# Reordered work at the seams of a two-block transformer kernel on one core

## The reference, cut to what matters

```python
for layer in range(2):
    mem_k, mem_v = split(mem @ w_mem_kv[layer])            # 256 memory tokens, 4 heads
    seq_out = hgrn2_mix(...) if layer == 0 else stick_breaking_attention(...)
    mem_out = memory_attention(qm, mem_k, mem_v)
    x = post_norm(x, concat(seq_out, mem_out) @ w_o[layer], ln_mix_g, ln_mix_b)
    x = post_norm(x, hier_moe(x, ...), ln_ffn_g, ln_ffn_b)  # 4 groups of 4 experts, 1 group and 2 experts per token
# second block
x = layer_norm_2(ALPHA_2 * x + fox_mixer(x, ...), ln_mix_g_2, ln_mix_b_2)
x = layer_norm_2(ALPHA_2 * x + conv_ffn(x, ...), ln_ffn_g_2, ln_ffn_b_2)
gate = sigmoid(x @ ple_w_gate + ple_b_gate)                 # 1024 x 1024
x = x + gate * (p @ ple_w_proj)                             # p: 256 tokens x 256, the small input
```

## Time and profile before

| what | value |
|---|---|
| median of 3 runs (lowest to highest) | 989.9 us (989.45 to 990.78) |
| profiled execution: its own time, its span | 992.38 us, 990.7 us |
| busy: PE, DVE, ACT, POOL | 97%, 73%, 57%, 4% of the span |
| read from HBM | 203.87 MB, 207 GB/s over the span |
| granted TensorE clock, mean | 0.996 of full speed |

### The profile page before, as it was taken

One profiled execution on the slowest core, in us unless ns is written; L12 is line 12 of the kernel. 1 busy time (PEld: TensorE's weight loads), 2 busy tenths in 40 slices (PEclk: granted clock), 3 DMA queues, 4 the chain that ended last, 5 costly groups with the idle time before them and its releaser, 6 DMA issues.

```text
span 990.7 us, 14556 instructions
## 1 busy us (share of the span) xinstructions
PE 959.4 (97%) x5530; PEld 818.1 (83%) x5530; DVE 727.5 (73%) x905; ACT 561.3 (57%) x629; POOL 37.8 (4%) x79
## 2 busy tenths in 40 slices
PE   8999989999999999999999999899999999999997
PEld 7978988888888779878888788679887788888886
DVE  4888885988898774645988888756565977777566
ACT  3845652577777644563677667624553756656441
POOL 8000010100000000001000000000000000000010
PEclk9999998999999999999999999999999999999999
DMA  9833336299989945431599899745452566555711
GB/s 321 278 111 128 128 100 199 79 323 356 306 302 359 357 155 186 160 96 43 170 339 342 274 352 359 256 128 185 157 191 85 183 201 205 175 175 203 250 52 42
DMA packets 151985, 205.82 MB, mean 208 GB/s; under 512 B 6896, under 2 KB 123376, under 8 KB 151920
## 3 DMA queue, kind: packets, MB, share of 16 engines
q1 hardware_dynamic: 150912, 204.24, 61.4%
q10 hardware_dynamic: 1008, 0.71, 0.2%
HBM read 203.87 MB, written 1.05 MB: 207 GB/s over the span
## 4 chain that ended last, share of the span: by engine, by line
PE 79%; DVE 10%; issue 4%; ACT 4%; DMA 2%; SPq 1%; POOL 0%; POOLq 0%; DVEq 0%; ACTq 0%
PE psum L638 77%; DVE w_lo L1961 3%; ACT w_hi L1493 1%; ACT arena L1493 1%; DMA raw<-in_a_w_in 1%; DMA raw<-in_attn_w_in 1%; DVE stats L2225 1%; SPq L281 1%; DVE x_res L2245 1%; PE psum L1117 1%; DVE x_res L2238 1%; DVE xt L1978 0%; ACT mt_hi L1493 0%; PE psum L1368 0%; DVE mt_lo L1978 0%
## 5 line engine op out<-in xcount | busy, mean ns | idle before, releaser
L1961 DVE TENSOR_TENSOR w_lo<-raw,w_hi 128x2048 fp32r<-128x2048 f32 x184 | 418.1, 2287 | 71.6 <-ACT w_hi L1493 69.8
L1493 ACT ACTIVATE w_hi<-raw 128x2048 fp32r<-128x2048 f32 (+1 forms) x186 | 353.9, 1905 | 105.0 <-PE psum L638 43.7
L638 PE MATMUL psum<-xt,w_hi 128*128 128x256 f32 (+1 forms) x1056 | 253.6, 321 | 3.8 <-DVEq L2709 1.7
L638 PE MATMUL psum<-xt,w_lo 128*128 128x256 f32 x704 | 197.1, 280 | 0.0
L638 PEld LDWEIGHTS psum<-xt,w_hi 128*128 128x128 f32 x1056 | 177.1, 190 | 20.3 <-issue 2.7
L638 PE MATMUL psum<-w_hi,mt_hi 128*128 128x512 f32 (+1 forms) x448 | 174.1, 389 | 0.2 <-issue 0.2
L638 PE MATMUL psum<-w_hi,mt_lo 128*128 128x512 f32 (+1 forms) x448 | 171.3, 382 | 0.0
L638 PE MATMUL psum<-w_lo,mt_hi 128*128 128x512 f32 (+1 forms) x448 | 171.0, 382 | 0.0
L638 PEld LDWEIGHTS psum<-xt,w_lo 128*128 128x128 f32 x704 | 133.6, 190 | 0.0
L638 PE MATMUL psum<-w_hi,xt 128*128 128x512 f32 (+1 forms) x368 | 115.2, 385 | 8.0 <-ACT mem_v L1493 3.7
L638 PEld LDWEIGHTS psum<-w_hi,mt_lo 128*128 128x128 f32 x448 | 84.2, 188 | 16.7
(11 more groups left out here) (252 smaller groups left out, 1024.1 us busy)
## 6 DMA issues: line engine op xcount, KB each, us to landing
raw<-in_w_gate SPq DMA_DIRECT2D x64, 512.0 KB, 4.9
raw<-in_w_up SPq DMA_DIRECT2D x64, 512.0 KB, 6.1
raw<-in_w_down SPq DMA_DIRECT2D x64, 512.0 KB, 6.0
raw<-in_ffn_w_up SPq DMA_DIRECT2D x44, 512.0 KB, 4.6
raw<-in_a_w_in SPq DMA_DIRECT2D x26, 512.0 KB, 6.9
raw<-in_attn_w_in SPq DMA_DIRECT2D x24, 512.0 KB, 5.9
raw<-in_ffn_w_down SPq DMA_DIRECT2D x22, 512.0 KB, 4.0
raw<-in_w_o SPq DMA_DIRECT2D x16, 512.0 KB, 4.6
```

What stands on the lines that cost most here:

```text
L638: return pe.matmul(o, l, r, start=start, stop=stop, skip_group_check=skip)
L1493: return act.activation(o, i, f, **kw)
L1961: return dve.tensor_tensor(w_half(h, w_lo), w_half(h, raw), w_half(h, w_hi).bitcast(F32), ALU.subtract).then_inc(lo_split, 1)
```

## The change

What it does, in the order of the diff below:

1. SP no longer loads ln_ffn_g and ln_ffn_b after the experts; ACT issues both loads right after it has rounded block 1 of x.
2. Slots count from 1, and a token's slot number in groups not its own is 0; one comparison over 128 x 512 builds perm, and load_max is read straight from PSUM by the reduction. PE's fill in layer 1 ahead of the gather is 7 products, not 12.
3. In the first projection the free banks are awaited one by one, and ACT copies MV1 before it rounds set 5 and any further weights.
4. The last scatter goes half by half over both blocks, and moe_done is counted for each pair of block and half; norm measures each half as it comes.
5. The small input p is transposed into bank 7 after C_Q0 and split into ht_hi and ht_lo in the attention; it leaves finish_projection and norm.
6. From u = 7 on, the projection's block 1 comes one turn earlier, and ACT and DVE round and rest the next two halves at u = 8. norm 4 rests no weight between its steps, and splits block 0 after it has shifted block 1. The fill behind the products of p waits for pp_out and is 5 products, not 6.
7. In the recurrence the logs of step 4 and the scaling of step 3 come ahead of a weight rest.
8. At the gate, one weight rest stands ahead of the scaling of block 1 and one between scaling and shift; the transposes of block 1 come inside tile 1; the fill ahead of tile 0 is 1 product, not 4; the last tile's bias is put into its bank by a product of ones, and ACT takes the sigmoid straight from PSUM.

```diff
@@ sync
-                gains(a["ln_ffn_g"][layer], a["ln_ffn_b"][layer], 2 * layer + 1)
@@ gpsimd
-            own.did(pool.iota(slot_no[:], pattern=[[1, P]], base=0, channel_multiplier=0,
+            own.did(pool.iota(slot_no[:], pattern=[[1, P]], base=1, channel_multiplier=0,
@@ tensor
+            def turn_p():
+                pe.wait_ge(p_in, 16)
+                for c in range(2):
+                    for b in range(TB):
+                        last = pe.transpose(psum[:, 7, T * c + P * b:T * c + P * b + P],
+                                            p_in_t[:, b, P * c:P * c + P], ident[:])
+                last.then_inc(tr_done, 1)
@@ project
-                for b in range(TB):
-                    free(f"O0{b}")
+                split_ready(s)
                 for half, j in ((0, 0), (0, 1)):
-                    split_ready(s + half)
                     for b in range(TB):
+                        if j == 0:
+                            free(f"O0{b}")
@@ finish_projection
-                    if layer == 2 and j == 0:
-                        pe.wait_ge(p_in, 16)
-                        turn(SETS["p"], p_in_t, 0, n=2)
@@ experts, layer 1
-                    keep_busy(12, 0)
+                    keep_busy(7, 0)
@@ scatter
-                        for b in range(TB):
-                            for n in range(2):
-                                if b == 0:
-                                    pe.wait_ge(s["y_hi"], of_group(i, q, n + 1, 2))
-                                    pe.wait_ge(s["y_lo"], of_group(i, q, n + 1, 2))
+                        for n in range(2):
+                            pe.wait_ge(s["y_hi"], of_group(i, q, n + 1, 2))
+                            pe.wait_ge(s["y_lo"], of_group(i, q, n + 1, 2))
+                            for b in range(TB):
...
-                            last.then_inc(sem("moe_done"), 1)
+                                last.then_inc(sem("moe_done"), 1)
@@ attention of the second block
             fm_half("C_Q0", xt_hi, xt_lo)
+            turn_p()
...
-                project_chunks(2, {6: (0, 1, 2), 7: (3, 4), 8: (5,), 9: (6,)}[u], 0)
-                if u >= 8:
+                if u in (7, 8):
                     pe.wait_ge(sem("fox_taken"), 6)
-                    project_chunks(2, O_ROWS[2][0], 1, (u - 8,))
+                    project_chunks(2, O_ROWS[2][0], 1, (u - 7,))
+                project_chunks(2, {6: (0, 1, 2), 7: (3,), 8: (4,), 9: (5, 6)}[u], 0)
...
-                last = row_block(AT["PP"], b, mt_hi[:, 0:2, :], mt_lo[:, 0:2, :], 4, True, True)
+                last = row_block(AT["PP"], b, ht_hi[:, 0, :, :], ht_lo[:, 0, :, :], 4, True, True)
...
-            keep_busy(6, 0)
+            pe.wait_ge(sem("pp_out"), 1)
+            keep_busy(5, 4)
@@ gate
+            def turn_second(k):
+                if k == 5:
+                    turn_block(SETS["L5"], 5, 1)
...
+            pe.wait_ge(sem("pl_bias_in"), 16)
             keep_busy(3, 4)
             turn_block(SETS["L5"], 5, 0)
-            keep_busy(4, 4)
+            mm(psum[:, GATE_BANK[-1], 0:LAST_WIDTH], ones[0:1, :], pl_bias[0:1, D - LAST_WIDTH:D], True, False, skip=True)
+            keep_busy(1, 4)
             gate_tile(0)
-            turn_block(SETS["L5"], 5, 1)
-            for n in range(1, len(GATE_TILES)):
+            gate_tile(1, turn_second)
+            for n in range(2, len(GATE_TILES)):
                 gate_tile(n)
@@ scalar
                 round_x(1)
+                for i, v in enumerate((a["ln_ffn_g"], a["ln_ffn_b"])):
+                    act.dma_start(gain[:, i, :], v[layer].rearrange("(o d) -> o d", o=1).to_broadcast([P, D]))\
+                        .then_inc(gain_in, 16)
                 round_to(base + 3)
...
+            act.wait_ge(half_used, AT["MV1"] + 1)
+            fn(mem_v[:, 1, :, :].rearrange("p m c -> p (m c)"), psum[:, 3, :], ACT.Copy).then_inc(drained_a, 1)
             split_set(5)
-            copy_unit("MV1", mem_v[:, 1, :, :].rearrange("p m c -> p (m c)"), 3)
...
+            act.wait_ge(tr_done, SETS["p"] + 1)
+            fn(ht_hi[:, 0, :, :].rearrange("p k t -> p (k t)"), psum[:, 7, :], ACT.Copy).then_inc(tr_hi, 1)
...
-            round_to(AT["UP"] + 1)
-            split_set(SETS["p"], n=2)
+                elif u == 8:
+                    round_to(AT["O2"] + 6)
...
+                    act.wait_ge(sem("gate_done"), n + 1)
+                    fn(s, psum[:, GATE_BANK[n], 0:width], ACT.Sigmoid).then_inc(sem("pl_gate"), 1)
@@ vector
-                    if 3 <= st + 1 < N_STEPS:
+                    if 3 <= st + 1 < N_STEPS and st != 3:
                         a_logs(st + 1)
-                    if st >= 3:
+                    if st >= 4:
                         a_scale(st)
...
+                if n == 0:
+                    a_logs(4)
+                    a_scale(3)
                 if h < A_HALVES[-1]:
                     split_to(h + AHEAD)
@@ norm
-                    if b and n != 5:
+                    if b and whole:
                         split_block(then, 0)
+                    if b:
                         split_to(between)
                     scale(b)
+                    if b:
+                        split_to(scaled)
                     shift(b)
+                if n == 4:
+                    split_block(then, 0)
...
-                return lambda b: dve.wait_ge(sem("moe_done"), 2 * layer + b + 1)
+                return lambda b, c: dve.wait_ge(sem("moe_done"), 4 * layer + 2 * c + b + 1)
@@ place, place_slots
-                own.link(dve.tensor_copy(r_pos.rearrange("p n g -> p (n g)"), psum[:, 6, 0:12]))
-                own.link(dve.tensor_reduce(r_mx, r_pos[:, 2, :], AX, ALU.max))
-                own.link(dve.tensor_copy(load_max[:], r_mx))
-                dve.nop().then_inc(sem("placed"), 1)
-                place(layer, None)
+                dve.tensor_reduce(load_max[:], psum[:, 6, 8:12], AX, ALU.max).then_inc(sem("placed"), 1)
+                own.link(dve.scalar_tensor_tensor(r_at.rearrange("p b g -> p (b g)"), psum[:, 6, 0:8], 1.0,
+                                                  rt[:, 64:72], ALU.add, ALU.mult))
+                place(layer, 0)
...
+                if u == 8:
+                    split_to(AT["O2"] + 5)
-            norm(4, ALPHA_2, projected(2), then=SETS["L4"], upto=AT["UP"] + 1)
+            norm(4, ALPHA_2, projected(2), then=SETS["L4"])
...
-            norm(5, ALPHA_2, downed, then=SETS["L5"], upto=HALVES)
+            norm(5, ALPHA_2, downed, then=SETS["L5"], between=AT["PG"] + 3, scaled=HALVES)
```

More of the change, by code:

```diff
@@ L1175, in experts @@
                             group(i, q, True)
-                    for b in range(TB):
-                        for c in range(2):
-                            last = mm(psum[:, 2 * b + c, :], zeros_r[:], zeros_row, False, True, skip=True)
-                        last.then_inc(sem("moe_done"), 1)
+                    for c in range(2):
+                        for b in range(TB):
+                            mm(psum[:, 2 * b + c, :], zeros_r[:], zeros_row, False, True, skip=True)\
+                                .then_inc(sem("moe_done"), 1)
                 with pe.Else():
@@ L1459, in _, with gate_tile @@
                     down_block(j, b)
-            def gate_tile(n):
+            def gate_tile(n, after=nothing):
                 b, at, width = GATE_TILES[n]
@@ L2211, in _, with norm @@
             split_to(AT["O0"] + 2)
-            def norm(n, alpha, ready, then, whole=False, between=0, upto=0):
+            def norm(n, alpha, ready, then, whole=False, between=0, upto=0, scaled=0):
                 first = 3 + 2 * n
@@ L2248, in norm @@
                 for b in range(TB):
-                    ready(b)
                     if whole:
-                        measure(b, 0)
-                        measure(b, 1)
+                        for c in range(2):
+                            ready(b, c)
+                            measure(b, c)
                     else:
+                        ready(b)
                         add(b, 0)
@@ L2278, in ready @@
                     h = AT[f"O{layer}"]
-                    split_to(h + ((6, 6), (5, 5), (5, 5))[layer][b])
-                    if b and layer == 2:
-                        split_set(SETS["p"], n=2)
+                    split_to(h + ((6, 6), (5, 5), (6, 6))[layer][b])
                     if b == 0:
@@ L2303, in place @@
             def place(layer, pair):
-                for b in range(TB):
-                    for q in range(2):
-                        g = slice(q, q + 1) if pair is None else bass.ds(pair * 2 + q, 1)
-                        last = dve.tensor_scalar(perm[:, b, P * q:P * q + P], slot_no[:], r_pos[:, b, g],
-                                                 r_og[:, b, g], ALU.is_equal, ALU.mult)
-                last.then_inc(sem(f"perm_ready{layer}"), 1)
+                at = r_at[:, :, 2 * pair:2 * pair + 2].rearrange("p b (q o) -> p b q o", o=1)
```

(6 more changed lines are left out.)

35 lines of the change are left out of this document (20 added, 15 removed).

## The result

The changed kernel takes 977.73 us (median of 4 runs, 976.75 to 979.18) against 989.81 us on the same chip; the ratio is 0.9869, 95% interval 0.9855 to 0.9883. The forecast was 977.1 us. The profiled execution has a span of 976.8 us (before 990.7).

The account below looks back on a forecast made before the run. TensorE, busy 97% of the span, was taken as the bound; terms 6.55 + 0.75 + 1.3 + 1.1 + 0.35 - 0.35 + 1.4 + 1.7 = 12.8 us off 989.9 gave 977.1 us, 8-in-10 range 973.5 to 982.3 us.

Parts of the forecast that it names:

- Part 1: First projection: copying memory values first saves 3.66 us of stall and 2.9 us of slow clock, 6.55 us.
- Part 2: First layer's recurrence: step 3 scaled ahead of a weight rest, 0.75 us saved.
- Part 3a: Expert ends: first statistic runs while PE adds the second half, 0.65 us in each layer, 1.3 us.
- Part 3b: Expert ends: scale and shift rows loaded earlier, so weights arrive sooner; 1.1 us over both layers.
- rival D: Slower: each issue on ScalarE's queue holds it until the rows have landed; 994.9 us, chance 0.03.
- Parts 4 to 7: Slots 0.35 us, small input in the attention -0.35 us, last projection 1.4 us, gate tiles 1.7 us.
- A: Clock falls once more, before the feed-forward or still in the first projection, costing 2.9 us: 980.0 us, chance 0.11.
- B: Only the large stall at the first projection goes, the small terms give nothing: 983.3 us, chance 0.08.
- C: Experts take the upstream gain back as weights come at fixed times, 7.65 us lost: 984.8 us, chance 0.05.

Follow-up runs that it names:

- mem_v_back: Changed kernel with ScalarE's old order at the first projection (set 5, a weight half, then the copy); 978.69 us, ratio 0.9886.
- copy_back: Changed kernel with ScalarE's old order and both free banks awaited ahead of the first projection's first product; 984.62 us, ratio 0.9930.
- copy_back_filled: Changed kernel with ScalarE's old copy order, both banks awaited, and 16 products of zeros ahead of that wait; 983.57 us, ratio 0.9924.
- gains_back: Changed kernel with the scale and shift rows back on SP's queue at the end of each expert layer; 980.50 us, ratio 0.9887.
- mem_v_only: Kernel before with only the memory values copied first on ScalarE and the free banks awaited one by one; 986.23 us, ratio 0.9956.
- copy_and_gains_only: Kernel before with memory values first, banks one by one, and scale and shift rows early on ScalarE's queue; 984.56 us, ratio 0.9933.
- stall_filled: Changed kernel with ScalarE's old copy order plus 16 products of zeros by TensorE ahead of the first projection; 981.21 us, ratio 0.9913.
- fill_twelve: Changed kernel with 12 products of zeros instead of 5 ahead of the feed-forward loop; 978.15 us, ratio 0.9854.
- ends_back: Changed kernel with the small input, the last projection and the gates as before; 981.50 us, ratio 0.9899.

## Why the prediction was right

**Part 1.** Stall and clock were right in size (3.95 and 2.82 against 3.66 and 2.9 us). The start came 0.3 us sooner, as the copy was over while the transposes ran. The reason given was half the story: "Afterwards the copy stands ahead of both" names ScalarE's order, while waiting for the banks one by one hides the late copy but for 0.68 us (mem_v_back). With both undone the stall is back (copy_back); whether ScalarE's order alone would do was not run. That the clock's price belongs to the stall is shown by copy_back_filled; that it is 2.9 us is true of one execution, and 1.58, 2.40 and 2.82 us are what three showed. One reading was thinner than I took it for: the window of the earlier trace rows ends at 777.40, just before the product behind the wait of 1.67 us. The window behind it does bear the argument out:

```profile
777.40:787.40 10.00, 9.96 (x57) 8.77 (x58) 8.08 (x7) 6.83 (x7) 0.00 (x0) 1.00 0.99 327
```


**Part 2.** 0.95 against 0.75 us, with the new wait at step 4 (0.36 us, forecast about 0.5).

**Part 3a.** From the last scatter's first product to the transposes it takes 5.35 us in both layers, before 5.82 and 5.85 us: 1.0 us in all against 1.3. The mechanism is the one forecast. VectorE's rest of the last half's sums (first row below, kernel before; second row, changed kernel) is now followed by the first statistic at once, and only the second waits 0.28 us for PE. From the start of that rest to the end of both statistics it takes 2.28 us, before 2.88 us: 0.60 us in each layer, forecast 0.65.

```profile
633.63 0.69 DVE L1978 TENSOR_TENSOR mt_lo<-psum,mt_hi 128x512 fp32r<-128x512 f32 x1 [0.56 <-ACT mt_hi L1493]
...
621.05 0.69 DVE L2003 TENSOR_TENSOR mt_lo<-psum,mt_hi 128x512 fp32r<-128x512 f32 x1 [0.67 <-ACT mt_hi L1508]
```

**Part 3b** is the term that does not fit: 1.1 us. I counted the wait that names the hidden half at the very end of layer 1 (0.67 us and the transpose ahead of it), and that wait is gone. But layer 1's experts and norm gave 3.4 to 4.6 us where 3a and 3b had 1.5. In the kernel before, two more waits of layer 1 stand where ScalarE waits for weights, 0.87 us at 547.38 and 0.99 us at 625.95, and they are gone too. The first can't be the rows' doing, as these are issued 66 us later:

```profile
547.38 0.44 PE L1117 MATMUL psum<-ident,arena 128*128 128x128 f32 x2 [0.87 <-DVE arena L2467]
...
613.89 0.34 SPq L338 DMA_DIRECT2D gain<-in_ln_ffn_g  x1
```

In the second profile of the same kernel the two are 0.39 and 0.74 us, and with late rows in gains_back both are gone. So they are not shown to be the rows'. What the runs do show is that early rows give 3.0 us of the stretch when they come alone and about 1 us beside the other edits, from one profile each and with a scatter of up to 2 us; how the rest comes about stays open. The issues on ScalarE's queue cost nothing, as forecast, so rival D is out. The Trainium skill ("DMA: Bandwidth & Descriptors", "Issuing engines are not separate DMA queues") says that another issuing engine saves only issue time; gains_back is in line with it: what moves is the wait for attn_w_in, 3.45 us with late rows and 0.68 us with early ones. But it changes the issuing engine and the time together, and no run changed the engine alone.

**Parts 4 to 7.** For the slots the two pairs give 0.10 and 0.74 us because TensorE's wait at the branch varies. Without that wait, the way from layer 1's counts to the branch takes 8.29 to 8.30 us in the four profiles with the old slots and 7.78 to 7.80 us in the ten with the new ones: 0.50 us against 0.35, and nothing in layer 0, as forecast. For the rest: -0.41 against -0.35 for the small input; 1.60 against 1.4 for the last projection, with 0.35 us of new wait where 0.6 was forecast and 1.73 us ahead of the loop where I had said 1.9; 1.77 against 1.7 for the gates.

**Not foreseen.** The feed-forward loop lost 2.35 us at an unchanged clock and list of work. It nearly cancels what layer 1's experts gave beyond their term. The forecast's 12.8 us met 12.1 us of median and 13.8 us of span partly by that luck. What sets the pace was not found. It stayed the same in two profiles of each kernel (346.7 ns before, 353.3 ns after). It was 346.7 ns in mem_v_only, copy_and_gains_only, mem_v_back and stall_filled, 353.3 ns in the six others. It is not the idle time ahead of the loop (fill_twelve) nor the edits to the last projection (ends_back), and mem_v_back differs from the changed kernel in three lines of ScalarE's list alone.

**Rivals.** A: in the changed kernel's two profiles the clock is at 1.00 from 20 to 940 us. But the mean clock is 0.998 in 2 of its 10 timed executions, 979.18 and 979.92 us, and in 13 of the 66 of all kernels without the stall. Each such execution is slower than the mean of those at 1.000 of its kernel, by 0.5 to 3.5 us. So in a part of the executions the clock most likely falls once more (0.2% of 977 us is some 2 us). No profile of the changed kernel caught one; copy_back_filled shows a possible place, the branch, which the prediction had not thought of. B: the small terms all stand in their own stretches. C: the gain at the projection reaches the end in the profile of mem_v_only. D: see 3b.

## What to carry over

A stall has as many cures as it has ends: before crediting a reordering on the producing engine, look whether the consumer can take first what is already free, and undo both before saying what either was worth. Where the list of work is the same, subtract stretch by stretch between fixed events; it tells 0.05 us where the medians here tell 2 us, and it finds gains and losses in places that nobody edited. Take the waits that vary out of the stretch first, and take two profiles of each kernel, since where weights are awaited the same code differs by up to 2 us. Two edits that relieve the same stretch need not add: try each alone and both together before giving either a price.

## What the runs showed of the hardware

- The idle stretch of 3.70 us was followed by 1.2 GHz for a varying time: mean granted clock over the next 6.1 us 0.50, 0.58 and 0.72 in three profiles, at a price of 2.82, 2.40 and 1.58 us. Products of zeros in its place left the clock at 1.00.
- After shorter idle stretches the clock mostly stayed: at 1.00 behind 0.83, 1.67, 1.73, 1.89 (mem_v_only) and 2.45 us (copy_back); but behind one of 2.47 us (copy_back_filled) it was 0.74 over the next 6.1 us, at a price of some 1.5 us.
- TensorE's wait at the branch after the gather (nothing in the profile releases it) took 1.06 to 2.47 us for the same code in fourteen profiles; in the changed kernel 1.55 and 1.46 us in one execution, 1.13 and 1.16 us in the next. Differences there of less than 1 us are not the edit's.
- A run of 704 products (352 pairs) went at one of two paces, 346.7 or 353.3 ns for a pair, at a granted clock of 1.00. It was the same in both profiles of the two kernels that were profiled twice. At the slower pace every third pair is some 11 ns longer than the two before it.
